# First stages of a two-block fp32 kernel: products with a diagonal of roots, another bias transfer, moved memory norms

## The reference, cut to what matters

```python
h = rmsnorm(x, norm_mix_g)
cb, cc, cx, q, k, v, gc, ga = split(h @ w_in)
y_conv = (cb * causal_conv3(cc * cx)) @ w_conv_out
logits = q k^T / 8 + rel_bias[t5_bucket(q_pos - k_pos)]      # causal, 8 heads of two maps
out = (softmax(logits_1) - lam * softmax(logits_2)) @ v
y_attn = (rmsnorm(out per head of 128, subln_g, eps=1e-5) * (1 - lam_init)) @ w_attn_out
merged = sigmoid(gc) * y_conv + sigmoid(ga) * y_attn
x = x + merged @ w_mix_out
x = x + cross_attention(rmsnorm(x), rmsnorm(mem), w_cq, w_ckv, w_co)
x = x + peer_ffn(rmsnorm(x))                                  # 16 experts for each of 8 heads
```

## Time and profile before

| | us |
|---|---|
| times of three runs | 1853.44, 1851.62, 1853.57; median 1853.44 |
| the profiled execution's own time | 1849.03 |
| its span, first to last instruction | 1847.1 |
| PE busy, DVE busy, ACT busy, POOL busy | 1546.8, 1150.0, 736.0, 248.4 |

### The profile page before, as it was taken

One profiled execution on the slowest core, in us unless ns is written; L12 is line 12 of the kernel. 1 busy time (PEld: TensorE's weight loads), 2 busy tenths in 40 slices (PEclk: granted clock), 3 DMA queues, 4 the chain that ended last, 5 costly groups with the idle time before them and its releaser, 6 DMA issues.

```text
span 1847.1 us, 20636 instructions
## 1 busy us (share of the span) xinstructions
PE 1546.8 (84%) x7910; PEld 1153.6 (62%) x7910; DVE 1150.0 (62%) x2004; ACT 736.0 (40%) x1333; POOL 248.4 (13%) x271
## 2 busy tenths in 40 slices
PE   7798988799888777777777777767899998789998
PEld 6688977798687223222332222236699878569987
DVE  5248778864557666766676676447654558854354
ACT  4244564424333333333333333333445335444532
POOL 0000000000002333333333333310000000000000
PEclk9899999899999999999999999988999999999999
DMA  5663335254248999999999999942155553114563
GB/s 216 160 227 137 141 134 183 75 185 151 91 160 312 423 421 422 422 421 422 421 412 422 422 415 411 423 193 91 69 182 180 186 182 121 46 69 174 182 192 114
DMA packets 71746, 443.66 MB, mean 240 GB/s; under 512 B 6975, under 2 KB 9279, under 8 KB 26208
## 3 DMA queue, kind: packets, MB, share of 16 engines
q0 software_dynamic: 36864, 268.45, 35.1%
q1 hardware_dynamic: 29888, 163.59, 25.6%
q10 hardware_dynamic: 4896, 10.31, 2.1%
HBM read 439.17 MB, written 3.15 MB: 239 GB/s over the span
## 4 chain that ended last, share of the span: by engine, by line
PE 51%; DMA 25%; DVE 15%; ACT 5%; issue 3%; ACTq 0%; POOL 0%; DVEq 0%
PE banks L906 23%; DMA arena<-experts,xn 22%; PE banks L935 15%; PE banks L1172 8%; DVE w_lo L1297 3%; DMA scratch<-arena 2%; DVE arena L1713 2%; DVE arena L1579 1%; PE banks L1039 1%; PE banks L1026 1%; ACT w_hi L520 1%; ACT xn L778 1%; DVE xn L1385 1%; DVE arena L1857 1%; ACT xn L782 1%
## 5 line engine op out<-in xcount | busy, mean ns | idle before, releaser
L1172 PE MATMUL banks<-arena,xn 128*128 128x512 f32 x1024 | 478.4, 612 | 157.8 <-ACT xn L782 156.3
L1297 DVE TENSOR_TENSOR w_lo<-raw,w_hi 128x2048 fp32r<-128x2048 f32 x154 | 352.1, 2290 | 294.8 <-PE banks L906 126.2
L1172 PEld LDWEIGHTS banks<-arena,xn 128*128 128x128 f32 x1024 | 187.1, 192 | 448.8 <-ACT xn L782 256.0
L1713 DVE CUSTOM_DVE_ANT_0 arena<-arena,banks 128x1024 f32<-128x1024 f32 x256 | 312.3, 1220 | 213.4 <-DMA arena<-experts,xn 210.9
L520 ACT ACTIVATE w_hi<-raw 128x2048 fp32r<-128x2048 f32 x154 | 292.9, 1907 | 209.3 <-PE banks L935 125.6
L495 POOL DMA_INDIRECT arena<-experts,xn x256 | 241.1, 942 | 452.2 <-PE banks L1172 384.9
L906 PE MATMUL banks<-op_hi,w_hi 128*128 128x256 f32 x1520 | 229.1, 292 | 18.0 <-ACT op_hi L579 10.5
L906 PE MATMUL banks<-op_hi,w_lo 128*128 128x256 f32 x1520 | 219.9, 289 | 19.7 <-DVE w_lo L1297 19.7
L906 PEld LDWEIGHTS banks<-op_hi,w_hi 128*128 128x128 f32 x1520 | 203.2, 196 | 28.1 <-issue 18.0
L906 PE MATMUL banks<-op_lo,w_hi 128*128 128x256 f32 x1520 | 217.1, 286 | 0.0
L906 PEld LDWEIGHTS banks<-op_hi,w_lo 128*128 128x128 f32 x1520 | 201.2, 197 | 22.0 <-DVE w_lo L1297 22.0
(11 more groups left out here) (214 smaller groups left out, 1193.3 us busy)
## 6 DMA issues: line engine op xcount, KB each, us to landing
raw<-wstream SPq DMA_DIRECT2D x154, 1024.0 KB, 4.9
arena<-experts,xn POOLq DMA_INDIRECT x256, 13.3
scratch<-arena ACTq DMA_DIRECT2D x1, 2048.0 KB
arena<-scratch ACTq DMA_DIRECT2D x2, 1024.0 KB, 8.7
xn<-mem_in ACTq DMA_DIRECT2D x2, 1024.0 KB, 4.8
x<-x_in SPq DMA_DIRECT2D x1, 1024.0 KB, 5.8
arena<-keys_in ACTq DMA_DIRECT2D x1, 1024.0 KB, 5.1
out_dram<-x SPq DMA_DIRECT2D x1, 1024.0 KB, 4.0
```

The costliest lines, as they stand in the source:

```text
L1172: mm = pe.matmul(sums[:, n, :], diag[:, s, :], rows[:, s, D + n * CW:D + (n + 1) * CW], start=False, stop=False, skip_group_check=True)
L1297: dve.tensor_tensor(w_lo[:, n % LO, :, :], raw[:, n % RAW, :, :], w_hi[:, n % HI, :, :].bitcast(F32), ALU.subtract).then_inc(lo_ready, 1)
L1713: dve.tensor_tensor_reduce(u, u, token_rows[k // PAIRS][:, :, :], 1.0, 0.0, ALU.mult, ALU.add, dots[:, s:s + 1]).then_inc(dot_ready, 1)
```

## The change

1. Rooted norms: PE multiplies the rows directly by the diagonal of the roots, 16 fp32 matmuls that turn and scale at once; `spread_roots`, the copy and `norm_t` are gone. The product can't start before the roots are there. This holds for mix, mem, mem2, mixa and mixb.
2. All norms: ACT makes `op_hi` from PSUM with the gain as scale (two pieces of 256 columns per bank), DVE makes `op_lo` from PSUM in one operation (gain times bank minus `op_hi`).
3. Start: the constants, the vectors and `bc` have a semaphore each, x comes by two DMAs, the sums for lambda come later on DVE.
4. Bias: 384 columns are kept instead of 512. A DMA writes the 8 rows to DRAM once, a second one copies each row 128 times within DRAM at a pitch of 1536 bytes (1.5 MB), a third reads 1 MB back skewed. ACT's waits for them stand after k1, and after the high rows of the memory norm.
5. The norm of mem moves from behind the attention to between v's two chunks; mem_in and mem2_in are loaded earlier. The norm of mem2 moves to between cv's two chunks.
6. Gates: ACT copies the products and applies Sigmoid once to each gate of 128x2048; DVE's reciprocals are gone.
7. Sub-layer: PE gathers the 8 heads' means in 8 rows x 256 (`subm`), POOL takes the root by `pow` on 8x256, PE spreads them (`sub`), DVE scales `o_diff` from PSUM. ck0 and ck1 come first; ck2 lies between `subm` and `sub`, ck3 behind.
8. The means and reciprocals for the memory keys are put later, between and behind the halves of cout.

```diff
--- before.py
+++ after.py
...
-            for n in ("mix", "mem", "mem2", "cross", "ffn"):
+            rstd("mix")
+            rstd("mem")
+            pool.wait_ge(sub_means, 1)
+            pool.tensor_tensor(sub_root, sub_mean, small[0:HEADS, 14:15].broadcast_to([HEADS, S]), ALU.pow)\
+                .then_inc(sub_roots, 1)
+            for n in ("mem2", "cross", "ffn"):
                 rstd(n)
...
+            def high_rows(n, gain_, buf, k=0, tiles=range(4)):
+
+                for j in tiles:
+                    wait_misc(act, ("xT", n, j))
+                    if k:
+                        act.wait_ge(norm_lo, norm_pairs(n, k - 1) + j + 1)
+                    for f in range(2):
+                        t = 2 * j + f
+                        e = act.activation(op_hi[:, buf, t, :], misc_bank(("xT", n, j))[:, f * S:(f + 1) * S], ACT.Copy,
+                                           scale=gain(gain_)[:, t:t + 1])
+                    e.then_inc(norm_hi, 1)
...
+                    square(c, 0)
+                    high_rows(n, n, buf, 0, range(2 * c, 2 * c + 2))
+                    square(c, 1)
...
             misc_emptied(act, ("bias",))
-            head = P * (2 * S + 1)
-            act.dma_start(bass.AP(scratch.tensor, 0, [[head, HEADS], [2 * S + 1, P], [1, 2 * S]]),
-                          bias_row.unsqueeze(1).broadcast_to([HEADS, P, 2 * S])).then_inc(bias_out, 16)
-            for j in range(4):
+            head = P * BIAS_ROW
+            row_at = HEADS * head
+            act.dma_start(bass.AP(scratch.tensor, row_at, [[BIAS_ROW, HEADS], [1, BIAS_ROW]]), bias_row)\
+               .then_inc(bias_out, 16)
+            for j in range(2):
                 copy_lin(("k", j), k_diff[:, 2 * j:2 * j + 2, :])
             act.wait_ge(bias_out, 16)
-            for qb in range(TB):
-                act.dma_start(bias[:, :, qb, :], bass.AP(scratch.tensor, S - 1 - P * qb,
-                                                         [[2 * S, P], [head, HEADS], [1, S]])).then_inc(bias_in, 16)
-            for j in range(4):
+            act.dma_start(bass.AP(scratch.tensor, 0, [[head, HEADS], [BIAS_ROW, P], [1, BIAS_ROW]]),
+                          bass.AP(scratch.tensor, row_at, [[BIAS_ROW, HEADS], [0, P], [1, BIAS_ROW]]))\
+               .then_inc(bias_spread, 16)
+            for j in range(2, 4):
+                copy_lin(("k", j), k_diff[:, 2 * j:2 * j + 2, :])
+            act.wait_ge(mem_in_s, 16)
+            sum_squares("mem", xn)
+            for j in range(2):
                 copy_lin(("v", j), v_diff[:, j % 2, j // 2 * CW:(j // 2 + 1) * CW])
+            high_rows("mem", "mem", 1)
+            act.wait_ge(bias_spread, 16)
+            act.dma_start(bias[:, :, :], bass.AP(scratch.tensor, P - 1, [[BIAS_ROW - 1, P], [head, HEADS], [1, S]]))\
+               .then_inc(bias_in, 16)
+            for j in range(2, 4):
+                copy_lin(("v", j), v_diff[:, j % 2, j // 2 * CW:(j // 2 + 1) * CW])
+            act.wait_ge(squares, squares_of("mem"))
+            act.dma_start(xn[:, :, :], mem2_in.rearrange("(t p) d -> p t d", p=P)).then_inc(mem2_in_s, 16)
             for j in range(4):
                 copy_lin(("cx", j), u_conv[:, 2 * j:2 * j + 2, :])
-            xn_free("mix")
-            act.dma_start(xn[:, :, :], mem_in.rearrange("(t p) d -> p t d", p=P)).then_inc(mem_in_s, 16)
...
+            def gate_sigmoid(name, dst):
+                for j in range(4):
+                    lin_emptied(act, (name, j))
+                act.activation(dst[:, :, :], dst[:, :, :], ACT.Sigmoid).then_inc(gates_ready, 1)
+
...
             act.activation(sq[:, :, :], o_diff[:, :, :], ACT.Square).then_inc(sub_sq, 1)
-            high_rows("mem", 1)
-            for j in range(4):
-                wait_misc(act, ("sub", j))
-                src = misc_bank(("sub", j)).rearrange("p (a b) -> p a b", a=2)
-                t = slice(2 * j, 2 * j + 2)
-                chain(act, act.activation(sq[:, t, :], src, ACT.Ln, bias=small[:, 8:9]), act_chain)
-                empty_misc(act.activation(means[:, t, :], src, ACT.Identity, bias=small[:, 8:9]), ("sub", j))
-
-            act.activation(sq[:, :, :], sq[:, :, :], ACT.Exp, scale=-0.5).then_inc(sub_roots, 1)
-            xn_free("mem")
-            act.dma_start(xn[:, :, :], mem2_in.rearrange("(t p) d -> p t d", p=P)).then_inc(mem2_in_s, 16)
-            for j in range(4):
-                copy_lin(("ck", j), k_cross[:, 2 * j:2 * j + 2, :])
+            copy_lin(("ck", 1), k_cross[:, 2:4, :])
+            gate_sigmoid("gc", gate_c)
+            wait_misc(act, ("subm",))
+            e = act.activation(sub_mean, misc_bank(("subm",))[0:HEADS, 0:S], ACT.Identity, bias=small[0:HEADS, 8:9])
+            empty_misc(e, ("subm",))
+            copy_lin(("ck", 2), k_cross[:, 4:6, :])
+            misc_emptied(act, ("subm",))
+            act.sem_inc(sub_means, 1)
+            gate_sigmoid("ga", gate_a)
+            copy_lin(("ck", 3), k_cross[:, 6:8, :])
...
-            high_rows("mem2", 0, 0)
-            high_rows("mem2", 1, 1)
+                if j == 1:
+                    act.wait_ge(half_done, LAST[("ga", 3)])
+                    high_rows("mem2", "mem2a", 0, 0)
+            act.wait_ge(half_done, LAST[("cv", 3)])
+            high_rows("mem2", "mem2b", 1, 1)
...
+            def norm(n, src=x):
+
+                for j in range(4):
+                    b = fill_misc(("xT", n, j))
                     for tb in range(TB):
-                        at = (2 * j + f) * P
-                        mm = pe.transpose(b[:, f * S + tb * P:f * S + (tb + 1) * P], src[:, tb, at:at + P], ident)
...
+                        if j == 0:
+                            pe.wait_ge(root_ready, TB * ROOTED.index(n) + tb + 1)
+                        for f in range(2):
+                            at = (2 * j + f) * P
+                            mm = pe.matmul(b[:, f * S + tb * P:f * S + (tb + 1) * P], src[:, tb, at:at + P],
+                                           root_diag[:, tb, :], start=True, stop=True, skip_group_check=True)
+                    mm.then_inc(misc_full, 1)
...
-            for _ in range(2):
-                tokens(0)
+            tokens(0)
+            pe.wait_ge(mem_in_s, 16)
+            norm("mem", xn)
+            tokens(0)
...
-            pe.wait_ge(mem_in_s, 16)
-            norm("mem", xn)
+            features(1, **normed("mem"))
             pe.wait_ge(sub_sq, 1)
+            b = fill_misc(("subm",))
+            for h in range(HEADS):
+                mm = pe.matmul(b[0:HEADS, 0:S], mean_of[:, HEADS - 1 - h:2 * HEADS - 1 - h], sq[:, h, :],
+                               start=(h == 0), stop=(h == HEADS - 1))
+            mm.then_inc(misc_full, 1)
+            half_chunk(True, 1)
+            pe.wait_ge(sub_roots, 1)
             for j in range(4):
                 b = fill_misc(("sub", j))
-                pe.matmul(b, mean128, sq[:, 2 * j:2 * j + 2, :], start=True, stop=True).then_inc(misc_full, 1)
-            features(1, **normed("mem"))
-            features(1)
-            for _ in range(2):
-                tokens(1)
+                for e in range(2):
+                    h = 2 * j + e
+                    mm = pe.matmul(b[:, e * S:(e + 1) * S], ident[0:HEADS, h:h + 1].broadcast_to([HEADS, P]), sub_root,
+                                   start=True, stop=True, skip_group_check=True)
+                mm.then_inc(misc_full, 1)
+            half_chunk(True, 1)
+            tokens(1)
...
+            def low_row(n, gain_, buf, j, k=0, last=True):
+
+                dve.wait_ge(norm_hi, norm_pairs(n, k) + j + 1)
+                for f in range(2):
+                    t = 2 * j + f
+                    ins = dve.scalar_tensor_tensor(op_lo[:, buf, t, :], misc_bank(("xT", n, j))[:, f * S:(f + 1) * S],
+                                                   gain(gain_)[:, t:t + 1], op_hi[:, buf, t, :].bitcast(F32),
+                                                   ALU.mult, ALU.subtract)
+                ins.then_inc(norm_lo, 1)
+                if last:
+                    dve.wait_ge(norm_lo, norm_pairs(n, k) + j + 1)
+                    dve.sem_inc(misc_free[MISC["xT", n, j] % 4], 1)
...
-                    dve.tensor_scalar(root_diag[:, tb, :], ident, rs[:, tb:tb + 1], float(P), ALU.mult, ALU.mult)\
+                    dve.tensor_scalar(root_diag[:, tb, :], ident, rs[:, tb:tb + 1], None, ALU.mult)\
                        .then_inc(root_ready, 1)
-                low_parts(upto)
-                for j in range(4):
-                    wait_misc(dve, ("xT", n, j))
-                dve.wait_ge(roots_full, ROOTED.index(n) + 1)
-                empty_lin(dve.tensor_copy(root_rows, lin_bank(("roots", n))[:, 0:S]), ("roots", n))
-                lin_emptied(dve, ("roots", n))
                 for k, (g, buf) in enumerate(dsts):
...
-                           .then_inc(norm_rows, 1)
+                    low_parts(uptos[k])
```

(30 more changed lines are left out.)

224 lines of the change are left out of this document (90 added, 134 removed).

## The result

| | before | after |
|---|---|---|
| median of four runs | 1852.86 us | 1839.67 us |
| the profiled execution: span of its instructions | 1847.1 us | 1837.3 us |

A forecast was written before the change was run, and what follows sets the result against it. PE held half of the chain and DMA a quarter, so PE's stalls and slow clock in the first 410 us were priced. The terms summed to -40.0 us: 1813 us against the median 1853.4, range 1801 to 1838.

The forecast's parts named there:

- The new wait: Before `sub`, PE waits for POOL's pow on 8x256, taken as X = 8 us, plus release and clock: +12.3 us.
- rival E: At the wait before `sub`, pow's X is 25 to 48 us, time 1830 to 1853; chance 0.08.
- Behind the attention: Attention's end through mem2: cheaper sub-layer means -7.2, ck and cv window -3.9, mem2 window -4.5 us.
- Bias and memory norm: Window of v, 66.9 to 108.3: stalls from the bias write go, mem's norm comes in: -15.9 us.
- The lower price: Bias spread in DRAM: 0.080 us a packet assumed, of bounds 0.080 to 0.176, as its rows start aligned.
- the rule of the eight heads: Bias spread: an outermost dimension below 16 confines a DMA to that many engines; alone it would keep 35 us.
- rival C: In v, the bias stall stays and ACT is late for cx's `w_hi`: +15 us, 1828; chance 0.12.
- Start: Kernel's start: first product with the diagonal at 10.1 us, clock rising sooner: -2.2 us, between -2.4 and +0.4.
- Gates: DVE's reciprocals no longer delay PE: -1.2 us in the attention, -13.5 in the window ahead of cout.
- Later norms: Norms from cross on: -0.4 us each for four, some 2 in mixb, 0.3 in mixa: -3.9 in all.
- rivals D and E: Wait before `sub`: D, pow dear, slower from X = 48 us, up to 1882, chance 0.10; E, X 25 to 48, 0.08.

The follow-up runs named there:

- the roots by ACT: Kernel after, with the sub-layer norm's roots made by ACT (Ln, then Exp) in place of POOL's pow: 1795.97 us, ratio to before 0.9688.
- the version with the late spreading products: Kernel after, pow kept on POOL, the products that spread the roots and DVE's scaling of o_diff moved to just ahead of cout: 1794.78 us, ratio to before 0.9691.

## Why the prediction was wrong, step by step

**The step that failed is "The new wait": "between ends a factor of 100 apart I take X = 8".** X is 41.12 us. The bounds held it (0.7 to 77), and so did the place, the reason and who waits. The geometric mean of two bounds is no measurement, and here it was not the neutral choice it looked. The earlier trace rows held more than I took from them: a pow and a memset on the same 128x2 differ by 0.60 us. If that is all per column, pow on 256 columns is 77 us, if half of it is, 39. The runs say 0.40 fixed and 0.158 per column, so 0.32 of the 0.70 were per column, and 128 x 0.32 + 0.40 is 41.4. I had called exactly this (rival E, X of 25 to 48, 1830 to 1853) the least likely case, 0.08, and cut the range off inside it, at 1838. The result, 1839.67, lies 1.7 us above the range.

The other numbers of that term: PE waited 0.2 us beyond POOL, not 0.8, since ACT's release at L724 went out while its copy of ck2 was still running. The low clock cost 5.7 us, not 3.5: `sub` took 7.19 us in place of 3.4 and ck3 7.62 in place of 5.76. In all the term is +47.0 in place of +12.3, and that accounts for the miss up to mixo: 17.8 + 16.8 = 34.6 against 34.7. But only 43.4 of the 47.0 go with the wait, as the roots by ACT show. The other 3.5 are low clock at `sub` and ck3 that stood there without a wait, and *Behind the attention*, which priced `sub` at the full clock, had no term for them.

*Bias and memory norm* was right, -16.0 against -15.9, cx beginning at 87.6 us at the full clock. **Its reason was half wrong.** I put the old write's 0.235 us a packet down to the pitch of 2052 bytes. The run from SBUF with aligned rows shows 0.216, the one with a pitch of 1540 from DRAM 0.084: the source was it, eight SBUF rows read 128 times each. The lower price that I chose was right for the wrong reason, which is luck, and even it was too high (0.080 against 0.067 measured). The spread took 17 us, where the rule of the eight heads taken alone would have kept 35. Nobody waited for it, and rival C fell.

*Start* gave -4.6 where I had -2.2 with a bound of -2.4. I had left out that the change loads x in two pieces, so that ACT squares the first while the second is under way: the norm began at 8.94 us, not 10.1. My times for the clock's rise there were read from the pace of the rows alone; the granted clock in the profile is 1.00 for the whole start, in both kernels, though in the kernel before a group of eight takes 1.91 us at 19.3 us and 1.12 from 22.4 on.

*Gates* and *behind the attention*: -1.5 against -1.2 in the attention. From its end to mixo, with the 47.0 taken out, -29.2 against -29.1. Put back one by one, the gates cost 9.3 us between `sub` and mixo and the keys 5.0 up to mixo, so the 13.5 hold up. But I put them to DVE's list ahead of cout alone. The keys' 5.0 are 1.21 and 1.39 us of PE's waits for ACT's roots of the key means and 2.39 for w_lo, and the first two stand in the kernel before with the same lengths: 2.6 us of the gain come from moving the key means, and not from DVE. The two lists together were not tried. In the kernel after PE waits within cout and aout for nothing but this, in aout:

```profile
392.94 1.22 PE L924 MATMUL banks<-op_hi,w_lo 128*128 128x256 f32 x8 [0.49 <-DVE w_lo L1320]
```

The 0.9 us forecast for it were 0.49.

*Later norms* gave -5.5 against -3.9. Cross gave 2.5 (0.4 forecast), mixa 1.2 (0.3), mlpa 0.9 and mlpb 1.0 (0.4 each), mixb 2.1 (2) and ffn nothing (0.4), and 0.7 came from the expert stage, which the change doesn't touch. Against this stands a loss of 2.9 us for which I had no term. It lies in the attentions of the last block. Windows over the same instructions in the kernel before, after, and with the bias transfer alone:

```profile
1593.86:1632.96 39.10, 29.16 (x160) 22.69 (x160) 29.44 (x97) 20.17 (x65) 0.00 (x0) 1.00 0.00 1
```

```profile
1582.10:1624.13 42.03, 33.06 (x159) 25.86 (x160) 29.41 (x97) 20.30 (x65) 0.00 (x0) 0.88 0.00 1
```

```profile
1573.83:1616.64 42.81, 34.17 (x159) 27.26 (x160) 29.49 (x97) 20.28 (x65) 0.00 (x0) 0.86 0.00 1
```

DVE and ACT do the same work in the same time; PE takes 3.9 us more for its own, at a granted clock of 0.88 in place of 1.00. The third kernel has the old norms and all else of before, and has the slow stretch too. So it isn't the new norms. The other nine profiles of the study have it too, 42.0 to 42.1 us at 0.88: the profiled execution of before was the only one of the twelve without it. That it explains most of the 3.8 us by which that execution lay under its median is likely, but no second profile of before was there to show it.

The signs and the chances: faster had 0.88, and faster it is, but by luck in good part: it came out through rival E, which gave 0.06 of the 0.88, with an X only 7 us short of the 48 at which my own sum has the sign turn. The formula that I gave for rivals D and E, slower from X = 48 us, would put X = 41.1 at 1853.4 - 52.3 + 0.8 + 3.5 + 41.1 = 1846.5; the measured 1839.7 is 6.8 under it. The start and the later norms make 4.0 of that, the release 0.6, the clock takes 2.2 back, and the 3.8 us by which the profiled execution of before lay under its median is most of the rest.

## What to carry to other kernels

A price that one row of two columns can't split is a reason for a range that reaches both ends, and for looking at what an engine does per column before it is given an instruction of 256 of them; here some 60 multiplications on the same 256 columns would have cost POOL no more than this one pow. An operation whose price is unknown goes where ten halves lie between it and its user, as the version with the late spreading products has it: then its price doesn't matter. And when a part of a change removes a transfer that everyone queues behind, run that part by itself: here it was worth 21 us, more than the whole change had left after its new wait.

## What the runs showed of the hardware that I had not expected

- pow on POOL takes 0.158 us per column and 0.40 fixed, 1.1 to 1.2 us more on 32 or 128 partitions than on 8 from 16 columns up; a multiplication 2.3 ns per column. 2048 roots as 8x256 take 41.1 us; by the row of 128x16 they would take 4.1 us.
- A DMA that reads the same few SBUF rows again and again takes 0.216 us for a packet of 1.5 KB; the same packets from rows in DRAM take 0.067. A row pitch that is off by 4 bytes takes this to 0.084.
- ACT loaded a table for Ln and another for Exp, 1.28 us each, in two instructions that followed one another.
- After 41 us without a matmul PE ran `sub` and the first two groups of ck3, 10.7 us, at the lower of its clock levels before its rows went back to 1.12 us a group.
- With no wait at all before `sub` (the roots by ACT) `sub` and ck3 still ran at a granted clock of 0.73 in the mean, 3.5 us longer than at the full clock; with `sub` moved behind ten halves it ran at 1.00.
- POOL computing pow for 41.12 us and DVE making low halves beside it, 2.29 us each from two operands in SBUF, did not lengthen one another.
- The same instructions of the last block ran at a granted clock of 1.00 in one execution and 0.86 to 0.88 in the eleven others, 2.9 to 3.7 us apart: a profiled execution can lie that far from its kernel's median with no edit at all.
